# Even attention of a two-block model as a three-step pipeline of query blocks, with score and value matmuls issued in turns on halves of the array

## What is computed

```
proj = h @ w_in                                   # 528 x 3080
# heads a (4, "differential"): q and k have two maps of 64, v has 128
p_a  = softmax(mask(q_a k_a^T / 8 - slope*|i-j|)) # for each of the two maps
o_a  = (p_a[map 0] - lam * p_a[map 1]) @ v_a      # then rms norm, gain
# heads b (8, "forgetting"): q, k, v have 64
cum_f = cumsum(log_sigmoid(f + bias))
p_b  = softmax(mask(q_b k_b^T / 8 + cum_f[i] - cum_f[j]))
o_b  = p_b @ v_b
out  = concat(o_a, o_b) @ w_out
```

## Time and profile before

| | |
|---|---|
| median of 3 runs | 3032.32 us (3021.95 to 3033.28) |
| profiled execution, its own time | 3036.59 us |
| its span, first to last instruction | 3034.6 us |
| mean granted clock of TensorE | 0.951 |
| TensorE matmul busy | 2886.1 us, 95% |
| VectorE, ScalarE, GpSimd busy | 1298.6, 1027.8, 302.1 us |
| even attention, first scores to last values | 35.09 to 396.69 us |

### The profile page before, as it was taken

How to read it: one execution, slowest core, us unless ns; L and a number is a source line. 1 busy time by engine, 2 the same in 40 slices (tenths; PEclk the granted TensorE clock), 3 DMA queues, 4 the chain that set the end, 5 groups by cost and what they waited for, 6 DMA issues and landing times.

```text
span 3034.6 us, 40015 instructions
## 1 busy us (share of the span) xinstructions
PE 2886.1 (95%) x16594; PEld 2484.7 (82%) x16594; DVE 1298.6 (43%) x2200; ACT 1027.8 (34%) x1612; POOL 302.1 (10%) x347
## 2 busy tenths in 40 slices
PE   8999999999999999999999999998988799999997
PEld 6877689999988888888888888887876687888886
DVE  4443345333442233255434433335467653543333
ACT  4432234322232222234332332223456533432221
POOL 0000021000120000030000300003122130300002
PEclk9888689999999999989999999999999999999998
DMA  3101022322212121123222142221311121242220
GB/s 127 42 15 42 28 77 98 105 91 91 70 43 67 55 94 56 63 77 129 94 98 90 36 152 92 96 89 58 119 56 49 43 83 42 78 138 91 97 70 28
DMA packets 66532, 232.87 MB, mean 77 GB/s; under 512 B 8880, under 2 KB 9264, under 8 KB 65968
## 3 DMA queue, kind: packets, MB, share of 16 engines
q1 hardware_dynamic: 66352, 230.31, 22.8%
HBM read 228.15 MB, written 2.10 MB: 76 GB/s over the span
## 4 chain that ended last, share of the span: by engine, by line
PE 81%; DVE 7%; ACT 5%; POOL 3%; issue 2%; DMA 1%; SPq 0%; DVEq 0%; POOLq 0%; ACTq 0%
PE ps L534 69%; PE ps L696 2%; PE ps L785 2%; PE ps L554 2%; POOL R L2347 2%; PE ps L664 1%; PE ps L667 1%; PE ps L565 1%; PE ps L772 1%; POOL S L2336 1%; PE ps L544 1%; DVE HT L1691 1%; ACT HT L1091 1%; DVE XL L1681 1%; DVE WL L1644 1%
## 5 line engine op out<-in xcount | busy, mean ns | idle before, releaser
L534 PE MATMUL ps<-XH,WH 128*128 128x264 f32 (+2 forms) x1856 | 552.2, 341 | 14.7 <-DVE XL L2310 7.7
L534 PE MATMUL ps<-XL,WH 128*128 128x264 f32 (+2 forms) x1856 | 537.5, 333 | 0.0
L534 PE MATMUL ps<-XH,WL 128*128 128x264 f32 (+2 forms) x1856 | 535.1, 331 | 0.0
L534 PE MATMUL ps<-XH,LENT 128*128 128x512 f32 (+2 forms) x2096 | 524.9, 343 | 6.3 <-DVE XL L1681 6.1
L534 PE MATMUL ps<-HH,LENT 128*128 128x264 f32 (+2 forms) x2220 | 497.4, 321 | 7.5 <-DVE HL L1651 7.5
L1644 DVE TENSOR_TENSOR WL<-RAW,WH 128x1024 fp32r<-128x1024 f32 (+1 forms) x232 | 287.4, 1239 | 276.8 <-ACT WH L1061 276.4
L534 PEld LDWEIGHTS ps<-XH,LENT 128*128 128x128 f32 x2096 | 356.9, 191 | 56.6 <-DVE XL L1681 9.0
L534 PEld LDWEIGHTS ps<-HH,LENT 128*128 128x128 f32 x2220 | 366.6, 193 | 37.6 <-issue 7.7
L534 PEld LDWEIGHTS ps<-XH,WH 128*128 128x128 f32 x1856 | 334.0, 198 | 53.2 <-issue 17.2
L534 PEld LDWEIGHTS ps<-XH,WL 128*128 128x128 f32 x1856 | 331.7, 197 | 28.7
L534 PEld LDWEIGHTS ps<-XL,WH 128*128 128x128 f32 x1856 | 332.6, 198 | 26.6
(11 more groups left out here) (220 smaller groups left out, 2947.0 us busy)
## 6 DMA issues: line engine op xcount, KB each, us to landing
RAW<-in_wf SPq DMA_DIRECT2D x128, 512.0 KB, 3.3
RAW<-in_wr SPq DMA_DIRECT2D x48, 512.0 KB, 3.2
RAW<-in_wg SPq DMA_DIRECT2D x44, 512.0 KB, 3.3
RAW<-in_wu SPq DMA_DIRECT2D x44, 512.0 KB, 3.2
RAW<-in_wd SPq DMA_DIRECT2D x32, 512.0 KB, 3.3
RAW<-in_we SPq DMA_DIRECT2D x24, 512.0 KB, 3.9
RAW<-in_wm SPq DMA_DIRECT2D x24, 512.0 KB, 3.3
RAW<-in_wro SPq DMA_DIRECT2D x16, 512.0 KB, 3.3
```

Source lines behind the costliest of these rows:

```text
L534: mm = e.matmul(o[:, at:at + m], wt, xt[:, k, c0 + a * m:c0 + (a + 1) * m], start=(n == 0 and j == 0), stop=(n == nk - 1 and j == 2))
```

## The change

- **Three steps.** Scores of block u = 5t + i, scaling of block u - 1 (VectorE, `even_probs`), turns of block u - 2 (TensorE, ScalarE). The probabilities have three buffers a map instead of two. The pipeline runs over the tiles' borders: turns of i = 3 and 4 and the values of a tile stand in the next tile, those of tile 7 after it.
- **Maps in turns.** For each piece of columns: map 0, map 1, and for fox then gate 0, gate 1. `e_CQ` and `e_CK` now are two full buffers, zeroed, with the gate at partition 64·mp and 64·mp + 32, so that each gate matmul is 64 deep and on its map's half. One signal for both maps.
- **Values.** Fox: both heads' matmuls in turns, each with 64 columns of v, on column halves 0 to 63 and 64 to 127, in one pair of banks, copied to HH and HL by one instruction each.
- **Turns** of 0 to 16 and of the rest in one row of blocks; ScalarE copies them all in one instruction; VectorE's 16-row copies are gone.
- **Panels.** In tile t: v of t, then q and k of t + 1, 4 steps after each block's scores, one ahead of the values and three at the end. `even_turn_v(t)` stands at i = 3. Tile 7 has its own v (2 steps each time). The weights' order follows. The forget matmuls come ahead of v 0.
- **Norm** of tile t - 1 cut in two: row sums at i = 2 of tile t, broadcast at i = 3. ScalarE copies the values to `TMP[3]`, and VectorE scales from there with the broadcast in PSUM, without a copy of it.
- **Banks.** Scores of up to 512 columns, turns of i < 4 and row sums take single banks out of 4 to 7 (`low=4`).
- **Ends.** The first two weo panels are moved ahead: seven steps, turns of (7, 3), seven steps, turns of (7, 4) and values 7, then their last steps. `ah.open`, which lets later weo splits into borrowed memory, is set after them.
- **Gates.** By `t % 2`: tiles 4 and 5 at once, 6 and 7 after `score[t - 2, 4]`, behind the weights of v(t - 1).

In the order of the file; `even()` is TensorE's, the call of `even_probs` VectorE's, the last lines SyncE's.

```
-    e_pb = [scr(TW) for _ in range(4)]
+    e_pb = [[scr(TW) for _ in range(2)] for _ in range(3)]
-    e_CQ = scr(2 * TW)[0:2, :].rearrange("p (s c) -> p s c", s=2)
+    e_CQ = [scr(TW) for _ in range(2)]
...
-            sets = [[i] for i in range(8)] if n == 1 else [[2 * i, 2 * i + 1] for i in range(4)]
+            sets = [[i] for i in range(low, 8)] if n == 1 else [[2 * i, 2 * i + 1] for i in range(4)]
...
+        def even_fill(t):
+            yield from even_panel(t, 8, S.v_copy)
+            if t < 7:
+                yield from even_panel(t + 1, 0, S.q_copy)
+                yield from even_panel(t + 1, 4, S.k_dve)
...
         def even_scores(t, i):
+            o = [bank(("score", t, i, mp), 1 if n <= 512 else 2, (S.soft, "max", t, i, mp), low=4) for mp in range(2)]
...
+            for at in range(0, n, 512):
+                m = min(512, n - at)
+                for mp in range(2):
+                    mm = e.matmul(o[mp][0:qn, at:at + m], e_q[t % 2][rows[mp], q0:q0 + qn], e_k[t % 2][rows[mp], at:at + m],
                                   start=True, stop=not fox)
+                if fox:
+                    for mp in range(2):
+                        mm = e.matmul(o[mp][0:qn, at:at + m], e_CQ[t % 2][rows[mp], q0:q0 + qn],
+                                      e_CK[t % 2][rows[mp], at:at + m], start=False, stop=True)
+            mm.then_inc(*S.score(t, i))
...
+        def even_values(t):
+            heads = 2 if t >= 4 else 1
+            wd = P // heads
+            freed = [(S.h_lo, "even", t, None)] if t >= 4 else [(S.sq, "even", t), (S.out_act, t)]
+            o = bank(("value", t), 2, *freed)
...
+                        for hh in range(heads):
+                            vt = e_VT[t % 2][0:kn, 128 * j + wd * hh:128 * j + wd * hh + wd]
+                            mm = e.matmul(o[wd * hh:wd * hh + wd, 512 * a + lo - a * HALF:512 * a + HALF], vt,
+                                          e_PT[pt][0:kn, j, lo:hi], start=(j == 0), stop=(j == 4 or (a == 0 and j == 2)))
...
+        def even_back(u, pump):
+            if u < 2:
+                return
+            t, i = divmod(u - 2, 5)
+            for mp in range(2 if t >= 4 else 1):
+                even_turn(t, i, mp)
+            if i == 4:
+                pump(1)
+                even_values(t)
+
+        def even():
+            drain(even_panel(0, 0, S.q_copy))
+            drain(even_panel(0, 4, S.k_dve))
+            even_forget()
+            norm = None
             for t in range(8):
+                pump = pumping(even_fill(t))
                 for i in range(5):
                     even_scores(t, i)
+                    if norm and i == 2:
+                        next(norm)
+                    if t < 7 or i < 4:
+                        pump(4 if t < 7 else 2)
+                    if i == 3:
+                        even_turn_v(t)
+                    if norm and i == 3:
+                        drain(norm)
+                        norm = None
+                    even_back(5 * t + i, pump)
+                    if i == 1 and 1 <= t <= 4:
+                        norm = even_norm(t - 1)
                 pump(100)
+            ends = [down_block("weo", m, "even", 0, TW) for m in range(2)]
+            for k in range(7):
+                next(ends[0])
+            even_back(40, pump)
+            for k in range(7):
+                next(ends[1])
+            even_back(41, pump)
+            drain(ends[0])
+            drain(ends[1])
+            down_norm("ln00", 2)
...
+                    even_scores(t, i)
+                    even_probs(5 * t + i - 1)
...
         gates(4)
+        gates(5)
+        for t in (6, 7):
+            weights_to(AT["we", even_index(t - 1, 8)] + 1)
+            gates(t)
```

More of the change, by code:

```diff
@@ L1169, in whole @@
             def whole():
-                for m in range(8 - n_end):
+                for m in range(done, 8 - n_end):
                     yield from ah.steps(name, base + m)
@@ new lines, in even_back @@
+        def even_back(u, pump):
+            if u < 2:
+                return
+            t, i = divmod(u - 2, 5)
+            for mp in range(2 if t >= 4 else 1):
+                even_turn(t, i, mp)
+            if i == 4:
+                pump(1)
+                w.wait_ge(*S.value[t])
+                if t >= 4:
+                    to_h("even", t, None, val(("value", t), TW), 0, TW)
+                else:
+                    tmp(2, S.h_lo, "even", t, None)
+                    e.activation(two(TMP[:, 2, :], TW), val(("value", t), TW), ACT.Square).then_inc(*S.sq("even", t))
+                    tmp(3, S.scaled, "even", t)
+                    e.activation(two(TMP[:, 3, :], TW), val(("value", t), TW), ACT.Copy).then_inc(*S.out_act(t))
@@ L1296, in even @@
+                    even_back(5 * t + i, pump)
+                    if i == 1 and 1 <= t <= 4:
+                        norm = True
+                pump(100)
+            ends = [ah.steps("weo", m) for m in range(2)]
+            for k in range(7):
+                next(ends[0])
+            even_back(40, pump)
+            for k in range(7):
+                next(ends[1])
+            even_back(41, pump)
+            drain(ends[0])
+            drain(ends[1])
             ah.open = AT["wro", 8]
-            down_norm("ln00")
+            down_norm("ln00", 2)
@@ new lines, in even @@
+                    if norm and i == 4:
+                        w.wait_ge(*S.scaled["even", t - 1])
+                        to_h("even", t - 1, None, two(TMP[:, 2, :], TW), 0, TW)
+                        norm = False
+                    even_back(5 * t + i, pump)
+                    if i == 1 and 1 <= t <= 4:
+                        norm = True
+                pump(100)
+            even_probs(39)
+            ends = [ah.steps("weo", m) for m in range(2)]
+            for k in range(7):
+                next(ends[0])
@@ L1944, in even @@
+            even_back(40, pump)
+            for k in range(7):
+                next(ends[1])
+            even_back(41, pump)
+            for m in range(2):
+                drain(ends[m])
+                residual("weo", m, m, 0, TW, None, ALPHA1)
             ah.open = AT["wro", 8]
-            down_norm("ln00")
+            down_norm("ln00", 2)
         def mlp(layer):
```

405 lines of the change are left out of this document (178 added, 227 removed).

## The result

The changed kernel takes 2942.8 us (median of 4 runs, 2939.7 to 2948.2) beside 3029.3 us for the kernel before on the same chip: ratio 0.9719, 95% interval 0.9693 to 0.9745, 86.5 us less.

A forecast was written before the change was run, and what follows sets the result against it. TensorE was taken to bound the stage, busy 339.99 of 361.6 us, some of it at low clock. Scores -31.6, values -10.6, panels +3, idle +6.3 gave -33; clock -15 made -48: 2984 us, range 2970 to 2997.

The forecast's parts named there:

- Clock: TensorE's time at 1.2 GHz in the even attention stage: 95 low us against 130 before, worth -15 us.
- clock near full: Rival: shorter scores and a filled tile 7 leave only single clock dips, -78 us, 2954 us; chance 0.17.
- Scores: Score and gate matmuls: paired passes save 27.2 us in tiles 4 to 7, 4.4 in tiles 0 to 3; -31.6 us.
- Values: Two fox heads' value matmuls in turns on column halves: 4.4 us a pair instead of 7.0, -10.6 us over four tiles.
- Panels: All 24 panels stay, but more groups of steps a tile mean some 19 more restarts: +3 us.
- Idle time: TensorE's waits in the stage for banks, gates and the end: 27.9 us against 21.6 before, +6.3 us.

The follow-up runs named there:

- b_gate64: Kernel before, with gates 64 rows deep on their map's half, map after map, banks of both maps taken ahead, one signal for both: 3023.95 us (0.9985).
- a_unboth: Changed kernel issuing map after map and head after head instead of in turns; pipeline, banks, 64-row gates and panels kept: 2967.28 us (0.9786).
- a_t7: Changed kernel with V7 back in tile 6 and the 14 weo steps out of the stage's end, so tile 7 has no panel: 2943.71 us (0.9714).
- i_p2: a_pipe2 with gate weights fetched earlier, the rest of a panel's steps before a tile's last turns, and row sums moved: 2918.81 us (0.9640).
- a_pipe2: Changed kernel with two pipeline steps instead of three: turns of block u - 1, not u - 2, behind the scores of block u: 2931.44 us (0.9666).
- a_t7_un: a_t7 with turns undone too: map after map and head after head, no panel in tile 7: 2972.71 us (0.9827).

## Why the prediction was wrong

The windows split the stage up to the third weo panel, in the two profiled executions. Before and after:

```profile
29.50:408.50 379.00, 357.39 (x1939) 280.63 (x1938) 153.63 (x552) 131.61 (x290) 0.63 (x1) 0.83 0.11 38
```

```profile
29.50:315.80 286.30, 253.22 (x1961) 221.43 (x1961) 128.24 (x481) 132.44 (x301) 0.00 (x0) 0.98 0.14 45
```

Of the 92.7 us, idle time is 33.1 - 21.6 = +11.5, busy time -104.2. In the stretches at 1.2 GHz TensorE was busy 125.7 us before and 11.6 after; half of that is what the clock cost, 62.8 and 5.8, so **clock -57**, and **work -47**. The medians differ by 10 us less; if work and idle time are the same in every execution, that puts the clock's part nearer to -50 between typical ones, an estimate.

| | forecast | measured |
|---|---|---|
| work (scores, values, restarts) | -39 | -47 |
| idle time | +6.3 | +11.5 |
| clock | -15 | -57 |
| sum | -48 | -93 in the profiled stage, -86.5 in the medians |

The step that failed is **Clock**: "I take 70. So 95 low us against 130", -15 us. It took 35 us of low time away, where the runs show 130 falling to 14. The case that came true is the rival *clock near full*, given 0.17, at 2954 us; work 8 us larger than forecast and idle time 5 us larger make up little of the rest.

- **Scores**, -31.6 forecast. The five blocks of a fox tile take 13.9 us before and 5.8 after (forecast 13.6 and 6.8), the differential i = 4 1.18 in place of 2.40 (1.3 forecast): -37. The size was near, the reason only in part: b_gate64 and a_unboth have some 30 of it without turns. That 512, 16, 512, 16 kept the maps apart is not so: a_unboth issues them in that order and takes 1.19 us.
- **Values**, -10.6 forecast, 4.4 us for a fox pair. 3.42 measured, so 4 x (7.0 - 3.42) = -14.3. The mechanism was right; the 0.2 us a matmul that I took over from the scores was not paid, and the earlier trace rows already spoke against it, with 3.5 us for one head's eight where 2.9 + 8 x 0.2 gives 4.5. The rule of the Trainium skill, "TensorE: Matmul & The Clock Gate", Part 3, that a weight load overlaps only where its row group differs, is not what this trace shows: both heads lie on the same rows, weight loads are busy for 2.15 of the 3.42 us in which matmuls have no gap, and the 32 records take less than 16 did.
- **Panels**, +3: -47 less -37 and -14 leaves +4 for restarts, as forecast.
- **Idle time**, 27.9 us forecast, 33.1 measured. The bank waits, forecast at 1.4, 0.7, 0.5, 0.6 and 0.25, came as 1.29, 0.54, 0.35, 0.73 and 0.17; the gates' stalls, 3.4 twice, as 4.38 and 3.50, with 0.85 ahead of tile 7; the end, 0.9 and 1.6, as 0.93 and 1.45. Not seen: up to 0.95 us ahead of a tile's first scores, which wait for the k copy, since k is now the last panel of the group; 2.4 us ahead of scores in tile 0, where 0.9 was forecast; and 1.86 us for V7.

Why the clock term failed: I took low time for something that stands beside waits and sparse work, tile by tile, and kept it where I put new waits. The runs speak against that. Tile 7 of the kernel before was idle for 0.6 of 42.6 us at 0.54, 25 us of a_t7's tile 7 21% idle without a panel at 1.00; i_p2 and a_pipe2 differ by 13 us of idle time and hardly in clock.

**Shown:** 14 us stayed low where 95 were forecast, and the low time around tile 7 (51 us before) is shortened by several edits, each by itself. In the old order each of these left part of it: a panel in the tile (some 20 us left), a panel ahead of it (27), turns and column halves (24). 64-row gates alone left all of it, with the pair of banks that they brought. In the new order the panels can be taken back with none of it returning in tile 7, and the turns with 10 us at most; both together bring back 7 us, and without the third step 20. These last three differ by no more than the scatter between executions; the distance from all of them to 51 is beyond it. **Open:** what these orders have in common. The place of a tile's scores ahead of the last turns of the tile before and of its values is in all of the good ones, as are 64-row or 33-row gates with the banks of both maps ahead, and values on column halves; undoing that place alone in the changed kernel was not tried, and the old order's bank waits with 64-row gates were not separated from it. So no mechanism of the clock is claimed.

## What to carry to other kernels

Price a change of order by work and idle time from the trace, and give the clock's share a wide range of its own that reaches to "all of it comes back": here it was 57 us of 93 in the profiled pair and decided the result. One profile of each kernel does not settle it: the same instructions had 3 us low in one execution and 17 in another. When a pipeline has cover for the softmax already, another step only adds waits for banks; count what lies between producer and consumer before deepening it. Before issuing two maps in turns, try the cheaper edit: with the gates on their map's own half and the banks of both maps taken ahead, map after map took the same time as turns up to 400 columns. After such a change read the waits by name: the 13.4 us removed between a_pipe2 and i_p2 moved the end of the stage by 14.8.

## What the runs showed of the hardware

- Two heads' float32 values on column halves, with weights on the same rows, in turns: 32 records in 3.42 us, against 3.50 for the 16 of one. Head after head on the same halves (a_unboth) they take 6.71.
- Scores and gates of two maps on their own row halves overlap without being issued in turns: at 400 columns 1.55 us, as with turns, where two-row gates on the lowest rows took 3.46; at 528 columns 4.06 us, where these took 5.49 and turns take 2.27.
- TensorE 98% busy for 42.6 us had a clock of 0.54, nearly all at 1.2 GHz (kernel before, tile 7), and TensorE 79% busy for 25 us stayed at 2.4 (a_t7, tile 7, with turns and halves as well as the new order). Without turns and with one head's values behind the other's, 84% busy for 36.75 us had 0.91 (a_t7_un). In these runs neither busy share nor the absence of gaps told the level.
